# The first mixer's projections as three fp32r products each, with weights split by ScalarE and GpSimd

## What is computed

```python
u = rms_norm(h, w_norm_mix)
proj = u @ w_in                       # conf_a, conf_g, z, xbc, dt_raw, gates
c = conf_a * sigmoid(conf_g)
c = silu(layer_norm(depthwise_conv(c, 31 taps)))
branch_conf = c @ w_conf_out
xbc = silu(depthwise_conv(xbc, 7 taps))
y = bidir_ssd(xs, dt_raw, ..., Bs, Cs, ssm_d)      # 32 heads, forward and backward scan
branch_ssm = rms_norm(y * silu(z), w_ssm_norm) @ w_ssm_out
merged = gates[:D] * branch_conf + gates[D:] * branch_ssm
h = h + merged @ w_out
h = h + expert_choice_ffn(rms_norm(h), ...)        # 16 experts
```

## Time and profile before

| | us |
|---|---|
| median of 3 runs (lowest, highest) | 2524.82 (2522.86, 2526.81) |
| the profiled execution's own time | 2524.76 |
| its span in the profile | 2522.7 |
| PE busy | 2373.0 (94%) |
| DVE busy | 1142.7 (45%) |
| ACT busy | 674.9 (27%) |
| POOL busy | 22.5 (1%) |

### The profile page before, as it was taken

The page is one execution under the profiler, slowest core; times in us unless marked ns, Lnnn a source line. Parts: engine busy times, 40 slices in busy tenths (PEclk is TensorE's granted clock), DMA queues, the critical chain, the costliest instruction groups (busy, mean ns, idle before and its releaser), DMA issues. The chain is left out here.

```text
span 2522.7 us, 34246 instructions
## 1 busy us (share of the span) xinstructions
PE 2373.0 (94%) x13937; PEld 1577.1 (63%) x13937; DVE 1142.7 (45%) x2374; ACT 674.9 (27%) x1213; POOL 22.5 (1%) x38
## 2 busy tenths in 40 slices
PE   8999999989999888888898879999999999999998
PEld 6786777874222222222222236889999999888887
DVE  5657973131111111111111116238887776788887
ACT  2125564020000000000000002324454444454444
POOL 1000000000000000000000000000000000000000
PEclk9999999989999999999989989899999999999999
DMA  5365556737999999999999991324775555777775
GB/s 172 107 217 172 177 171 203 242 140 300 405 428 428 428 428 427 428 427 428 428 428 428 428 369 35 133 84 140 222 228 175 179 174 178 249 241 243 242 242 162
DMA packets 205420, 677.03 MB, mean 268 GB/s; under 512 B 15072, under 2 KB 137200, under 8 KB 180336
## 3 DMA queue, kind: packets, MB, share of 16 engines
q1 hardware_dynamic: 205296, 675.30, 72.3%
HBM read 657.40 MB, written 17.83 MB: 268 GB/s over the span
## 5 line engine op out<-in xcount | busy, mean ns | idle before, releaser
L549 PE MATMUL ps<-u,ring 128*128 128x272 f32 x1248 | 298.7, 395 | 4.1 <-DVE ring L387 2.9
L984 PE MATMUL ps<-ring,tokens 128*34 128x512 f32 x1248 | 273.6, 593 | 16.6 <-DMA ring<-in_w_up 16.6
L549 PEld LDWEIGHTS ps<-u,ring 128*128 128x128 f32 x1248 | 233.1, 190 | 55.8 <-issue 8.7
L2019 PE MATMUL ps<-m_hi,row_hi 128*128 128x256 f32 x1024 | 256.4, 288 | 0.8 <-ACT peer_s L2085 0.8
L1162 DVE TENSOR_TENSOR first_room<-first_room,ps 98x512 f32<-98x512 f32 x32 | 21.8, 682 | 505.7 <-PE ps L984 505.7
L2019 PE MATMUL ps<-m_lo,row_hi 128*128 128x256 f32 x1024 | 250.7, 283 | 0.0
L984 PE MATMUL ps<-extra_early,tokens 128*34 128x512 f32 x752 | 197.4, 676 | 14.7 <-DMA extra_early<-in_w_gate 11.8
L984 PEld LDWEIGHTS ps<-ring,tokens 128*34 128x34 f32 x1248 | 72.2, 112 | 215.2 <-issue 185.5
L1001 PE MATMUL ps<-ring,first_room 128*34 128x512 f32 x768 | 179.6, 614 | 25.5 <-DVE first_room L1166 23.0
L2019 PEld LDWEIGHTS ps<-m_hi,row_hi 128*128 128x128 f32 x1024 | 195.7, 191 | 1.6 <-issue 1.0
L2019 PEld LDWEIGHTS ps<-m_lo,row_hi 128*128 128x128 f32 x1024 | 196.1, 191 | 0.0
(11 more groups left out here) (398 smaller groups left out, 3015.7 us busy)
## 6 DMA issues: line engine op xcount, KB each, us to landing
ring<-in_w_down SPq DMA_DIRECT2D x48, 2048.0 KB, 22.4
ring<-in_w_up SPq DMA_DIRECT2D x47, 2048.0 KB, 24.5
ring<-in_w_gate SPq DMA_DIRECT2D x31, 2048.0 KB, 24.7
extra_early<-in_w_gate SPq DMA_DIRECT2D x31, 2048.0 KB, 18.5
ring<-in_w_in SPq DMA_DIRECT2D x36, 1024.0 KB, 5.4
extra_early<-in_w_up SPq DMA_DIRECT2D x16, 2048.0 KB, 25.7
extra_early<-in_w_down SPq DMA_DIRECT2D x16, 2048.0 KB, 25.4
rows<-in_peer_u SPq DMA_DIRECT2D x64, 512.0 KB, 3.7
```

Of the source, the lines that this page charges most:

```text
L549: last = pe.matmul(bank[:, 0:T], wt[:, k, c:c + P], src[:, k, :], start=k == 0, stop=k == kt - 1)
L984: last = pe.matmul(s.ps[HALF * j:HALF * j + CAP, 2 * c + u % 2, :], s.tokens[:, 2 * (u // 2) + k, :], rows[k][:, 1024 * c + 512 * j:1024 * ...
L2019: pe.matmul(out, hi[:, P * k:P * k + P], m[:, k, :], start=k == 0 and m is s.m2_hi, stop=False)
```

## The change

Each product of the mixer's tiles, float32 weight W by float32 input X, becomes three fp32r products: W_hi X_hi + W_hi X_lo + W_lo X_hi. fp32r is a rounded float32 in the same four bytes.

- **Parts.** The weights are cut into 105 parts of 8 products: one for each tile, two for an ssm tile, and dt (half the size). For each part ACT rounds 128x1024 weights into one of two buffers (`round_weights(n)`, at L817 of the changed kernel), and GpSimd subtracts them from the weights in place (`lower_part`, L287 there); the first four parts are subtracted by DVE. ACT's stream has the rounding of part n+2 ahead of the evacuation of tile n. It waits for the weights, for PE's last use of the buffer (`hi_used`) and for the subtraction of part n.
- **Inputs.** u, the conf input, y and merged get upper parts by ACT (8, 8, 16 and 8 operations of 128x272; for y it takes the place of a scaling) and lower parts by DVE (as many). u's upper part lies over h, which is loaded again during the ssm tiles.
- **PE.** `proj(t)` makes 8 products W_hi X_hi, 8 W_hi X_lo, waits for the lower part and makes 8 W_lo X_hi.
- **Slots.** The two buffers of upper parts take the place of one slot of the ring, so three are left (`MIXER_RING = 3`), and SP loads unit i when unit i-3 was used.
- **Experts' loads.** Two of the four expert units (2 MB each) that SP issued among the ssm tiles now come behind the last ssm tile.

```diff
-            pool.wait_ge(cb_out, GROUPS)
-            pool.memset(s.decay[:, :, :], 0.0).then_inc(clean, 1)
+            for n in on_pool:
+                if parts[n][0] == pos["a", 4]:
+                    pool.wait_ge(cb_out, GROUPS)
+                    pool.memset(s.decay[:, :, :], 0.0).then_inc(clean, 1)
+                pool.wait_ge(w_hi, n + 1)
+                lower_part(pool, n).then_inc(w_lo, 1)
...
+    def lower_part(eng, n):
+        return eng.tensor_tensor(lower_view(n), weights_of(n), upper_part(n).bitcast(F32), ALU.subtract)
...
-            before = {tiles[pos["ssm", m]][2]: m - 1 for m in range(1, 5)}
+            before = {tiles[pos["ssm", m]][2]: m + 1 for m in range(1, 3)}
...
+                if i == tiles[pos["ssm", 3]][2]:
+                    sp.wait_ge(tiled, pos["gate", 2 * KT - 1] + 1)
+                    sp.dma_start(s.h[:, :, :], hT).then_inc(h_again, 16)
...
+            for u in range(AHEAD, AHEAD + 2):
+                s.load_expert_unit(sp, 0, u)
-            sp.wait_ge(tiled, pos["out", 3] + 1)
+            sp.wait_ge(tiled, pos["out", 5] + 1)
...
+            for k in range(KT):
+                dve.wait_ge(u_hi, k + 1)
+                dve.tensor_tensor(s.u_lo[:, k, :], s.u[:, k, :], s.u_hi[:, k, :].bitcast(F32), ALU.subtract)\
+                   .then_inc(u_lo, 1)
+            for n in on_dve[0:4]:
+                dve_lower(n)
...
-                    for k in range(kt):
-                        last = pe.matmul(bank[:, 0:T], wt[:, k, c:c + P], src[:, k, :], start=k == 0, stop=k == kt - 1)
+                    for n in parts_of[t]:
+                        k0 = parts[n][2]
+                        pe.wait_ge(w_hi, n + 1)
+                        for src, sem in ((hi, hi_sem), (lo, lo_sem)):
+                            for k in range(KT):
+                                if m == 0:
+                                    pe.wait_ge(sem, k0 + k + 1)
+                                last = pe.matmul(bank[:, 0:T], upper_part(n)[:, k, :], src[:, k0 + k, :],
+                                                 start=src is hi and k0 + k == 0, stop=False)
+                        last.then_inc(hi_used, 1)
+                        pe.wait_ge(*lower[n])
+                        for k in range(KT):
+                            last = pe.matmul(bank[:, 0:T], lower_view(n)[:, k, :], hi[:, k0 + k, :],
+                                             start=False, stop=n == parts_of[t][-1] and k == KT - 1)
...
+            def round_weights(n):
+                act.wait_ge(*w.ready[parts[n][1]])
+                if n >= 2:
+                    act.wait_ge(hi_used, n - 1)
+                    act.wait_ge(*lower[n - 2])
+                act.activation(upper_part(n), weights_of(n), ACT.Copy).then_inc(w_hi, 1)
+
             def evacuate(t):
                 kind, m, _, _ = tiles[t]
+                for n in parts_of.get(t, ()):
+                    round_weights(n + 2)
                 act.wait_ge(tiled, t + 1)
```

More of the change, by code:

```diff
@@ L253, in mixer, with lower_view, upper_part, weights_of @@
     first_pair_tile = pos["z", 0]
+    parts, parts_of = [], {}
+    for t, (kind, _, unit, c) in enumerate(tiles):
+        if unit is not None:
+            parts_of[t] = []
+            for k0 in range(0, IT if kind == "ssm" else KT, KT):
+                parts_of[t].append(len(parts))
+                parts.append((t, unit, k0, c, 64 if kind == "dt" else P))
+    on_dve = [n for n in range(len(parts)) if n < 4]
+    on_pool = [n for n in range(len(parts)) if n not in on_dve]
+    lower = {n: (w_lo_dve, i + 1) for i, n in enumerate(on_dve)}
+    lower.update({n: (w_lo, i + 1) for i, n in enumerate(on_pool)})
+    def lower_view(n):
+        _, unit, k0, c, width = parts[n]
+        return w.view(unit, s.t1_lower)[:, k0:k0 + KT, c:c + width]
+    def upper_part(n):
+        width = parts[n][4]
+        return s.w_hi[:, n % 2, 0:KT * width].rearrange("p (k c) -> p k c", k=KT)
+    def weights_of(n):
+        _, unit, k0, c, width = parts[n]
+        return w.view(unit)[:, k0:k0 + KT, c:c + width]
+    def lower_part(eng, n):
+        return eng.tensor_tensor(lower_view(n), weights_of(n), upper_part(n).bitcast(F32), ALU.subtract)
     square_rows = s.xbc[:, :, :].rearrange("p k t -> p (k t)")[:, 0:KT * T].rearrange("p (k t) -> p k t", k=KT)
@@ L523, in proj @@
                 kind, m, unit, c = tiles[t]
-                if unit is not None:
-                    wt = w.wait(pe, unit)
                 if t >= 2:
@@ L637, in _ @@
             last.then_inc(sum0, 1)
-            wt = w.wait(pe, tiles[0][2])
-            for k in range(KT):
-                pe.wait_ge(normed, k + 1)
-                for t in range(2):
-                    last = pe.matmul(ps[:, t, 0:T], wt[:, k, P * t:P * t + P], s.u[:, k, :], start=k == 0, stop=k == KT - 1)
-                    if k == KT - 1:
-                        last.then_inc(tiled, 1)
+            pe.wait_ge(w_hi, 2)
+            for src, sem in ((s.u_hi, u_hi), (s.u_lo, u_lo)):
+                for k in range(KT):
+                    pe.wait_ge(sem, k + 1)
+                    for t in range(2):
+                        last = pe.matmul(ps[:, t, 0:T], upper_part(t)[:, k, :], src[:, k, :], start=src is s.u_hi and k == 0, stop=False)
+                        if src is not s.u_hi and k == KT - 1:
+                            last.then_inc(hi_used, 1)
+            for t in range(2):
+                pe.wait_ge(*lower[t])
+                for k in range(KT):
+                    last = pe.matmul(ps[:, t, 0:T], lower_view(t)[:, k, :], s.u_hi[:, k, :], start=False, stop=k == KT - 1)
+                last.then_inc(tiled, 1)
             for t in range(2, pos["a", 0]):
@@ L844, in _ @@
             act.activation(s.std[:, :], ps[:, 7, 0:T], ACT.Sqrt, bias=s.eps[:, 0:1], scale=1.0 / INNER).then_inc(ystd, 1)
+            for m in range(5, KT):
+                round_weights(parts_of[pos["conf", m]][0])
+            for n in parts_of[pos["ssm", 0]]:
+                round_weights(n)
             for m in range(KT):
+                for n in parts_of[pos["ssm", m]]:
+                    round_weights(n + 2)
+                act.wait_ge(evac_d, KT + m + 1)
+                act.activation(s.m_hi[:, m, :], s.u[:, m, :], ACT.Copy).then_inc(m_hi, 1)
+            for m in range(KT):
+                if m + 2 < KT:
+                    round_weights(parts_of[pos["out", m + 2]][0])
                 act.wait_ge(evac_d, 2 * KT + m + 1)
```

108 lines of the change are left out of this document (82 added, 26 removed).

## The result

| | before | changed |
|---|---|---|
| median of 4 runs (lowest, highest) | 2525.82 (2522.86, 2526.97) | 2635.01 (2631.17, 2644.74) |
| ratio, 95% interval | | 1.044 (1.0408 to 1.0472) |
| span | 2522.7 | 2629.8 |

The runs of the kernel before are the three of the table ahead of the prediction and one more. The change makes the kernel 4.4% slower, by some 109 us. The forecast was 2569 (+44), its range ended at 2608: the direction is right, the loss is 2.5 times what was forecast.

The account below looks back on a forecast made before the run. The prediction took the mixer to be bound by PE, with DVE second; under exclusion of DVE and GpSimd, 65 - 24 + 3 = +44 on 2524.76 gave 2569, range 2462 to 2608.

Parts of the forecast that it names:

- Under exclusion the time of the two engines adds up: Mixer, 38 to 364 us: DVE's 250 plus GpSimd's 134 make 384 us where 326 are now, +58.
- costed at nothing: ACT's 105 roundings, 111 us at 1.06 each, fit beside the last 8 products of a tile: no cost.
- A: Rival, chance 0.60: the sum with DVE and GpSimd excluding each other, 2569, own range 2544 to 2605.
- B: Rival, chance 0.22: the engines don't exclude each other; PE's -66 + 5 and +4 in the pairs remain, 2468.
- The pace of PE: Mixer tiles: a part takes 3.04 us as 24 fp32r products against 3.67 as 8 float32 ones, saving 0.63.
- -66 us, where PE stays the bound: Mixer: PE's saving of 0.63 us a part over 104 full parts.
- I take 2.2: GpSimd's subtraction of a part's 1024 elements takes 2.2 us, as two one-input passes, under a tile's 3.04.
- 15.2 us: Length of a pair under exclusion, against 12.28 before; +37 over 12.75 pairs that have convolution.
- From there on PE is the bound again: -24 + 3: Last three pairs, conf, ssm and out: 38 parts give back 24 us, small terms add 3.
- Between +58 and +72 I take +65: Loss up to the end of the pairs with convolution, between the engines' summed time (+58) and the milestones (+72).
- C: Rival, chance 0.12: exclusion, but a subtraction of only near 1.1 us; 2525, between 2495 and 2540.
- D: Rival, chance 0.06: three slots are too few, without exclusion; ada units land late, +26 on B: 2494.

Follow-up runs that it names:

- e15: Changed kernel without subtractions, and without ACT's roundings from part 2 on or PE's waits for either, leaving the products alone (wrong weights): 2486.97 us, ratio 0.9853.
- e1: Changed kernel without subtractions: GpSimd and DVE clear one element instead, PE multiplies by a zero for lower weights; roundings and waits stay: 2524.25 us, ratio 0.9992.
- e3: Kernel before with three weight slots instead of four, nothing else but one expert unit's wait: 2525.76 us, ratio 1.0001.
- e11: Changed kernel with GpSimd subtracting only half of each part (128x512), which PE uses twice: 2556.42 us, ratio 1.0121.
- e4: Kernel before with three slots, plus 103 unused GpSimd subtractions of 128x1024 on a scratch slot, paced by PE's tiles: 2598.71 us, ratio 1.0292.
- e14: e1 with ACT's roundings cut to two elements a row from part 2 on, waits and order kept: 2502.56 us, ratio 0.9912.
- filled kernel: Two runs: e1 plus five zero products in each part, 2560.24 us; changed kernel plus 16 zero products ahead of each scan from the fourth pair, 2640.77 us.
- e10: Kernel before with three slots and three fp32r products only for conf, ssm and out, all 32 subtractions on DVE: 2518.98 us, ratio 0.9974.

## Why the prediction was wrong in size and right in sign

The forecast's own mechanism, DVE and GpSimd shutting each other out, was there. What failed is how its price was added up. "Under exclusion the time of the two engines adds up" laid the work of two engines end to end and left out that PE, ACT and DVE stand in turn while one of them waits: the first pair began 18 us later than forecast and the pairs took 24 us more. And ACT's roundings, "costed at nothing", cost 38 us where they could be measured, without the subtractions.

One can also divide the miss by rivals. The forecast had A 101 us above B; the subtractions measured 110, so exclusion as a whole was priced nearly right, and the kernel without it came at 2524 and not at B's 2468. The two ways share one miss and must not be added.

Step by step, as it put them:

- **The pace of PE: right.** 3.0 us a part (forecast 3.04); the tail of e15 gives back 16.0 of 20 - 3 forecast.
- **"-66 us, where PE stays the bound", and rival B's "0.3 x 12 = +4": wrong.** Products alone give 38. Ahead of the pairs -18.5 (forecast about -23), the tail -16.0 (about right), and in the pairs only -3.8 against -16. DVE's 11.0 us of work a pair were laid beside PE's 11.0 as if they ran without gaps; the measured pair is 12.06, since DVE also waits for ACT's decays and PE for DVE. Here the chain between two engines nearly level set the length of the pair, and not the larger of their sums. Of A's own sum this touches only the -24 at its end.
- **"ACT's 105 roundings ... costed at nothing": wrong, +38.** The duration was right (1053 ns against 1.06 us), but neither its time (+22) nor its place (+16) was free in the kernels without subtractions. The prediction asked only whether ACT has the time. It didn't ask what stands queued behind a rounding that waits for its weights two tiles ahead: the evacuations and decays, 48.7 us of such waits in e1. Three slots are enough where PE alone reads them (e3).
- **"I take 2.2" for GpSimd: near.** 2.41 us median, inside A's own 2.6.
- **"Under exclusion the time of the two engines adds up": right in kind, short in size.** The first mask came at 123.04 (forecast 120), the second convolution ended at 174.2 (174). DVE's first string of the long convolution ended at 219.45, and before it ended 15.9 us ahead of the first scan (184.62, 200.52): with that the first pair would have begun at 235.3, as forecast. It began at 253.2. So all of the missing 18 us come behind that string. The place, in timelines of the changed kernel:

```profile
204.27 22.02 POOL L287 TENSOR_TENSOR ring_parts<-ring,ring_parts 128x1024 fp32r<-128x1024 f32 x3 [6.44 <-ACT ring_parts L817]
...
202.87 16.58 DVE L377 SCALAR_TENSOR_TENSOR conf<-cpad,small,conf 128x272 f32<-128x272 f32 x40
...
206.59 1.16 PE L636 MATMUL ps<-u_lo,ring_parts 128*128 128x272 f32 x8
221.70 2.18 PE L641 MATMUL ps<-u_hi,ring_parts 128*128 128x272 f32 x8 [13.96 <-POOL ring_parts L287]
...
221.76 1.06 ACT L817 ACTIVATE ring_parts<-ring 128x1024 fp32r<-128x1024 f32 x1 [14.10 <-POOL ring_parts L287]
```

40 operations of DVE run on for 16.58 us, 0.41 us each, as if nobody else were there, and GpSimd's subtraction ends only after them. PE stands for 13.96 us for a 2.4 us operation, and ACT for 14.10. e11 has the same stand at the same place for a subtraction that is half as long:

```profile
195.11 2.18 PE L642 MATMUL ps<-u_hi,ring_parts 128*128 128x272 f32 x8 [13.06 <-POOL ring_parts L324]
```

So the time of the two does not just add up in any order: here DVE had a long string of work, PE waited for GpSimd, and what was left of the string landed on PE.
- **The pairs, "15.2 us": 16.8 on average** over the thirteen from 253.18 to 471.39, the starts of their scans; single ones took 14.6 to 18.6 (253.18, 271.78, 290.42; 407.13, 421.76). In e4, where no engine of the mixer waits for GpSimd and ACT rounds nothing, the same thirteen take 16.1 (223.67 to 433.27). First scan to conf +56.8, forecast +33 (37 for the pairs with convolution, less 4 for the last ones).
- **"From there on PE is the bound again: -24 + 3": -3.8 in the tail, not -17.** e1 already loses 5.2 of it to ACT (against e14), and the subtractions another 6.9; the lower part of y on DVE took 1281 ns, against 494 in e1.
- **"Between +58 and +72 I take +65": another 7.** The sum by milestones was the better one, though still short.

Over the forecast's +44 these make 18 ahead of the pairs, 24 in them, 13 in the tail and 7 by the choice between two sums: 62 of the 65 us that are missing. 1.7 more arise between the mixer's end and the experts' first product, and 2 are the difference between the medians (109.2) and the profiled executions (107.1).

One slip in the working changed nothing: A's own range has its upper end at 2605, but its terms give 2569 + 24 + 7 = 2600.

What no step had is **PE's clock**. It was 1.00 before, and 0.81 to 0.85 over 400 us in the changed kernel, where PE stood still again and again. It is part of all the numbers above. How much of the 110 us it makes by itself stays open: e4, with float32 products, loses 73 us at 0.95, 0.88 and 0.97 (in the stretches of the table above), and neither filled kernel raised it where it was lowest.

Of the rivals, B falls by its own test (the convolutions' mean rose to 652 and 681 ns), C by GpSimd's 2.41 us, D by e3. Of the signs of A, the pace of PE, the lengthened convolutions, some operations of 2 to 3 us and PE's waits were met. Three were not: GpSimd was busy 291.5 us (forecast 220 to 260), its mean was 2.9 us (2.2 or a little over), and the pairs stood 16.8 us apart and not 15. The first two are the hint of the rest: the work took what was forecast, and the waiting for a turn came on top.

## What to carry to other kernels

A faster product is worth only what its loop's next chain leaves: price it first with the products alone and nothing that feeds them (here 38 us of 66). A preparation step on an engine with room to spare can cost through what is queued behind it, even where its work would fit (here 38 us for 110 us of work on an ACT that was 27% busy). And keep GpSimd's reading operations away from a DVE with long strings of two-input work (here busy three quarters of the time in the middle of the mixer), above all where TensorE waits for them. In the tail, where DVE was busy 19.8 of 127.9 us before, three products with DVE's own subtractions gave back 12.6 us (e10), and with GpSimd's 3.8.

## What the runs showed of the hardware

GpSimd's wait for its turn was not bounded by one DVE operation. Timelines of the changed kernel, first POOL, then DVE, near 55 and near 141 us (the second POOL row holds two subtractions; the first of them took 9.98 us):

```profile
55.10 2.69 POOL L287 TENSOR_TENSOR ring_parts<-ring,ring_parts 128x1024 fp32r<-128x1024 f32 x1 [0.56 <-ACT ring_parts L817]
...
140.80 12.51 POOL L287 TENSOR_TENSOR ring_parts<-ring,ring_parts 128x1024 fp32r<-128x1024 f32 x2 [2.33 <-ACT ring_parts L817]
...
55.44 2.64 DVE L377 SCALAR_TENSOR_TENSOR xbc<-xpad,small,xbc 128x272 f32<-128x272 f32 x1
...
148.09 0.48 DVE L377 SCALAR_TENSOR_TENSOR xbc<-xpad,small,xbc 128x272 f32<-128x272 f32 x1
148.61 2.47 DVE L377 SCALAR_TENSOR_TENSOR xbc<-xpad,small,xbc 128x272 f32<-128x272 f32 x1
```

At 55.10 it got in within 0.34 us, and DVE's next operation took 2.64. From 140.80 DVE's operations went on every 0.41 us until 148.61, and only then did one take 2.47 us. What decides between the two wasn't found; the longest subtraction took 17.4 us. The Trainium skill (SBUF — State Buffer, section "SBUF: two separate sides") says that whichever starts first holds the ports for its instruction and the other blocks; the single holds agree (2.64 and 2.47 us), the passing over of a waiting GpSimd for some 19 DVE operations is more than it states.

Other numbers: an fp32r product of 128x128 by 272 columns 0.125 us at the upper level of the clock and 0.23 to 0.25 at the lower (1.2 GHz); a GpSimd subtraction with two inputs 2.41 us for 128x1024 and 1.35 for 128x512, and 1.89 us for 1024 where both inputs were the same row piece and the output was float32 (e4).
